# Where the rotated-partner copies of the first mixing linear stand in the request queue

## The reference, cut to what matters

```python
for l in range(DEPTH_2):                       # 2 layers
    h = rmsnorm(x, attn_norm[l])
    z = h @ w_in[l]                            # (512 x 1024) @ (1024 x 9420)
    (qA, kA, vA, fA, qB, kB, vB, qI, kI, wI,
     qC, kC, vC, gC, qD, kD, vD, gates) = jnp.split(z, split_at, axis=-1)
    yA = forgetting_attention(heads(qA, FOX_HEADS), ..., fA, forget_bias[l])
    yB = dsa_attention(rope(heads(qB, DSA_HEADS), pos), rope(kB[:, :, None], pos)[:, :, 0], vB,
                       rope(heads(qI, IDX_HEADS), pos), rope(kI[:, :, None], pos)[:, :, 0], wI)
    ...
    yD = sliding_window_gqa(rope(heads(qD, ...), pos), rope(heads(kD, ...), pos), heads(vD, ...), ...)
```

## Time and profile before

| | |
|---|---|
| median of three runs | 2974.98 us |
| the profiled execution, whole | 2973.03 us |
| its span, first to last instruction | 2971.2 us |
| mean granted TensorE clock | 0.998 |
| TensorE matmul busy | 2934.1 us (99% of the span) |
| VectorE busy | 1715.4 us (58%) |
| ScalarE busy | 1394.3 us (47%) |
| GpSimd busy | 1241.8 us (42%) |
| chain that ended last, by engine | TensorE 89%, VectorE 8%, ScalarE 2% |

### The profile page before, as it was taken

The page is one execution under the profiler, slowest core; times in us unless marked ns, Lnnn a source line. Parts: engine busy times, 40 slices in busy tenths (PEclk is TensorE's granted clock), DMA queues, the critical chain, the costliest instruction groups (busy, mean ns, idle before and its releaser), DMA issues.

```text
span 2971.2 us, 42626 instructions
## 1 busy us (share of the span) xinstructions
PE 2934.1 (99%) x16366; PEld 2454.2 (83%) x16366; DVE 1715.4 (58%) x2539; ACT 1394.3 (47%) x2318; POOL 1241.8 (42%) x870
## 2 busy tenths in 40 slices
PE   8999999999999999999999999999999999999998
PEld 7778888799988877788888888878787888878987
DVE  7974333497814978772117865178777511297732
ACT  6443344455533446663235545244566532354542
POOL 5336574410254533234555324454332354562243
PEclk9999999999999999999999999999999999999999
DMA  5334232233223422123323233244231233333322
GB/s 162 87 112 142 94 131 96 72 114 114 84 98 89 145 73 86 52 75 95 97 96 106 82 103 110 86 114 138 67 95 47 75 98 97 96 90 106 96 96 71
DMA packets 215047, 288.96 MB, mean 97 GB/s; under 512 B 42698, under 2 KB 122626, under 8 KB 213058
## 3 DMA queue, kind: packets, MB, share of 16 engines
q1 hardware_dynamic: 212354, 281.06, 31.2%
q0 software_dynamic: 880, 2.99, 0.3%
q10 hardware_dynamic: 1616, 2.23, 0.2%
HBM read 270.98 MB, written 4.72 MB: 93 GB/s over the span
## 4 chain that ended last, share of the span: by engine, by line
PE 89%; DVE 8%; ACT 2%; issue 1%; DMA 0%; POOL 0%; SPq 0%; ACTq 0%; DVEq 0%
PE half L914 69%; PE half L1243 3%; PE half L1246 3%; PE half L1245 3%; PE half L1402 2%; PE half L1416 2%; PE half L1380 1%; PE half L1385 1%; DVE arena L2546 1%; DVE arena L3523 1%; DVE qz L3523 1%; DVE arena L3037 1%; DVE wL L2569 1%; PE half L1478 0%; PE half L1169 0%
## 5 line engine op out<-in xcount | busy, mean ns | idle before, releaser
L3639 POOL TENSOR_TENSOR wL<-slot,wH 128x512 fp32r<-128x512 f32 (+1 forms) x840 | 1191.5, 1427 | 1700.2 <-ACT wH L1602 1665.5
L1602 ACT ACTIVATE wH<-slot 128x512 fp32r<-128x512 f32 (+1 forms) x840 | 515.9, 623 | 958.4 <-PE half L914 942.6
L914 PE MATMUL half<-arena_split,wH 128*128 128x512 f32 (+1 forms) x2432 | 736.0, 385 | 1.0 <-POOL wL L3639 0.6
L914 PE MATMUL half<-nH,wH 128*128 128x512 f32 x1792 | 709.5, 396 | 3.7 <-ACT arena L1615 2.3
L914 PE MATMUL half<-nH,wL 128*128 128x512 f32 x1792 | 698.6, 390 | 0.0
L914 PE MATMUL half<-nL,wH 128*128 128x512 f32 x1792 | 698.1, 390 | 0.0
L914 PEld LDWEIGHTS half<-arena_split,wH 128*128 128x128 f32 x2432 | 451.1, 188 | 93.8 <-POOL wL L3639 2.8
L914 PE MATMUL half<-arena_split,wL 128*128 128x512 f32 (+1 forms) x1216 | 466.4, 384 | 0.0
L914 PEld LDWEIGHTS half<-nH,wH 128*128 128x128 f32 x1792 | 336.4, 188 | 88.7 <-issue 18.2
L914 PEld LDWEIGHTS half<-nH,wL 128*128 128x128 f32 x1792 | 336.4, 188 | 71.6
L914 PEld LDWEIGHTS half<-nL,wH 128*128 128x128 f32 x1792 | 336.7, 188 | 67.9 <-issue 1.4
(11 more groups left out here) (424 smaller groups left out, 4542.4 us busy)
## 6 DMA issues: line engine op xcount, KB each, us to landing
slot<-in_w_in SPq DMA_DIRECT2D x344, 256.0 KB, 2.7
slot<-in_w_up SPq DMA_DIRECT2D x272, 128.0 KB, 2.2
slot<-in_w_down SPq DMA_DIRECT2D x132, 256.0 KB, 2.6
arena<-in_w_up SPq DMA_DIRECT2D x168, 128.0 KB, 2.4
slot<-in_w_branch SPq DMA_DIRECT2D x64, 256.0 KB, 2.7
slot<-in_w_out SPq DMA_DIRECT2D x48, 256.0 KB, 2.7
arena<-arena SPq DMA_DIRECT2D x40, 256.0 KB, 4.4
slot<-in_w_gate SPq DMA_DIRECT2D x48, 128.0 KB, 2.3
```

What stands on the lines that cost most here:

```text
L914: mm = pe.matmul(dst, lhsT, rhs, start=(k == 0 and m == 0), stop=(k == last and m == 2))
L1602: act.activation(wH[:, p, 0:cols], slot[:, s, 0:cols], ACT.Copy).then_inc(weights_high, 1)
L3639: pool.tensor_tensor(wL[:, p, 0:cols], slot[:, s, 0:cols], plainly(wH[:, p, 0:cols]), ALU.subtract)\
```

## The change

In each layer the four partner copies of `mix1` are asked for behind the first four units of `mix2` in place of behind all eight. Units 4 to 7 of `mix2` (sixteen requests) come behind the copies, ahead of qB units 4-7. The programs of the other four engines are the same.

```diff
                     load("b" + name, lin(w, r, c0), l, units=range(4))
+                    mix2 = cols((FOX_F, 8), (IDX_W, 4), (DSA_V, 64), (SWA_V, 128))
                     if name == "qB":
-                        load("bmix2", cols((FOX_F, 8), (IDX_W, 4), (DSA_V, 64), (SWA_V, 128)), l)
+                        load("bmix2", mix2, l, units=range(4))
                     if name in roped:
                         partners(*roped[name])
+                    if name == "qB":
+                        load("bmix2", mix2, l, units=range(4, KD))
                     load("b" + name, lin(w, r, c0), l, units=range(4, KD))
```

## The result

The changed kernel takes 2977.74 us (median of 21 runs, 2976.39 to 2980.14), the kernel before, in runs beside it, 2973.29 us (21 runs, 2972.28 to 2975.03). The ratio is 1.0014, 95% interval 1.0008 to 1.0021: slower, by 4.45 us between the medians. The forecast was +1.9 us and "no change". The time lies in the range, the sign and the place are as forecast, and the size is more than twice what was worked out; it is also just outside the "0.5 to 4" us that had most of the chance.

The account below looks back on a forecast made before the run. TensorE, busy for 99% of the span, was taken to bound the kernel. Losses of 1.7 us in layer 0 and 0.2 in layer 1, sum 1.9, on the median 2974.98 gave 2976.9 us; range 2974.0 to 2980.5.

Parts of the forecast that it names:

- 0.5 to 4: Whole kernel: the main forecast, slower by about 2 us within these limits in us; chance 0.72.
- The copies do not start earlier: SP, both layers: copy requests still begin when VectorE has emptied mix1, at 956.22 and 1970.34 us; gain 0.
- possible accident: Layer 1: VectorE's extra lag of 1.64 us behind the copy requests might come from traffic behind them; gain at most 1.50 us.
- What mix2 units 4-7 pay: Layer 0, behind the copies: sixteen requests at 0.475 us each make TensorE late at units 6, 7 and qB 4; 1.7 us.
- The bound of 2.4 for layer 0: Layer 0: upper bound of the loss in us, with GpSimd at 1.30 and 2.1 us for each subtraction.
- Layer 1 loses 0.2: Layer 1: the same 1.7 us late at qB unit 4, 1.5 covered; net 0.2 us, between -1.5 and 0.9.
- the 1.5 us of cover: Layer 1: TensorE already stood 1.50 us before index_dots, waiting for VectorE's rotation, so 1.5 us of lateness costs nothing.
- GpSimd blocked: Rival, units 6, 7 and qB 4: subtractions wait for whole VectorE operations of 2.2 us; 8.5 us in all, 2983.5; chance 0.05.
- The clock: Rival: new TensorE waits lower its granted clock in both layers, 1.7 us each; 2980.3 us; chance 0.03.
- SP held at every request: Rival: all sixteen requests take 1.20 us in place of 0.475; layer 0 11.7 late, layer 1 10.2; 2997 us; chance 0.02.
- Everything hidden: Rival: layer 0 loses 0.1, layer 1 nothing or gains up to 1.5; 2973.6 to 2975.1 us; chance 0.15.

Follow-up runs that it names:

- the two medians: The changed kernel timed twice against the kernel before, with no edit between: 2977.74 us beside 2973.29, then 2976.92 us beside 2973.52.

## Why the prediction was right in kind and short in size

**The copies do not start earlier: right.** They wait for VectorE's emptying of mix1 in both kernels. Their end does move, which the forecast took only for a possible accident. In layer 1 VectorE starts on them 8.55, 8.76 and 8.74 us after the first request in the three profiles in which that layer has the old order and undivided copies. It is 8.03, 8.22, 7.93 and 7.98 us in the four in which small pieces of mix2 stand right behind them. The most that index_dots had of this was 0.2 us, with the copies behind six units; with the copies behind four qB unit 4 came too late for it. Nor does what stands behind the copies land behind them: the first piece of mix2 in layer 1 is asked for at 1977.48 and lands 3.9 us later, at 1981.4, while VectorE waits for the copies until 1982.45.

**What mix2 units 4-7 pay: the mechanism was right, the size of layer 0 was not.** The worked sum said 1.7 us, and 2.8 was measured, in three profiles within 0.14 us. Unit by unit, units 5, 6 and 7 of mix2 and unit 4 of qB were to be 0, 0.6, 1.2 and 1.7 late, and were 1.4, 1.6, 1.8 and 2.8. The term that was too small is the request queue. I let SP be held twice just behind the copies and then go at 0.475 a piece. The request for the last piece of unit 5 was held a further 1.05 us. That made unit 5 late, which the prediction had as "just hidden", and all units behind it. GpSimd's 1.59 and 1.35 for units 4 and 5 against an assumed 0.63 and 0.85 did not matter but for 0.5 us at unit 5, since SP set the pace behind it. The bound of 2.4 for layer 0 was exceeded too: it had taken GpSimd at its slowest, but SP without another hold.

**Layer 1 loses 0.2: too small, by another term.** There the last piece of unit 7 is asked for 1986.09 - 1974.42 = 11.67 us after the first copy request, and the prediction had 967.9 - 956.22 = 11.7. What was off is GpSimd: 3.81 us for unit 7 and qB unit 4 where I took 1.1 + 1.5 = 2.6, with a pause of 0.3 between them. The narrow one waits for VectorE's operation that ends at 1989.63 and is over at 1990.10; the wide one waits for the next, which ends at 1991.18, and is over at 1992.32. So qB unit 4 is 2.7 late, not 1.7, and behind the 1.5 us of cover 1.2 is left, not 0.2. The cover itself was right. With these two terms put right the sum is 2.8 + 1.2 = 4.0, and the two medians are 4.45 and 3.40.

**The rivals.** GpSimd blocked (0.05): the mechanism was true and only its size was not. The prediction read the rows as "between no lock and a full one", and that reading was wrong. A subtraction waits for what is left of the operation under way, not for a whole one of 2.2 us: about 1.1 us each for the two in layer 1, which makes it 1.2 us late there in place of 5.0. In all twelve profiles the narrow subtractions that meet the rotation end 0.47 to 0.49 us after an operation of it (a few late ones, nearly past it, up to 0.60), and the wide ones 1.12 to 1.16 after. The Trainium skill, "SBUF — State Buffer", section "SBUF: two separate sides", says that whichever of the two starts first has the shared pair for the whole instruction and that the other fully blocks. The trace agrees. The clock (0.03): it did fall in layer 1, in one of two profiles of the changed kernel, at 1.6 us where the rows said 1.7. I had argued that the new waits were too small and too scattered; TensorE was busy for only 1.59 of 3.00 us, but so it was in the profile without the fall. SP held at every request (0.02): no, but one request in sixteen was held more than foreseen. Everything hidden (0.15): no; it is what happens with eight requests behind the copies.

## What to carry to other kernels

A request in a row of requests costs its issuing engine the same however few bytes it has, here 0.475 us from start to start for 2 to 256 KB. What matters when requests are moved is how many stand ahead of the first block that an engine wants, against how fast that engine uses blocks up. Before a wait is moved ahead of others, look at what ends it: this one ended at the same time wherever it stood, and only what was put behind it moved. Two engines that take turns must be counted as a pair: a subtraction of 0.63 us and a VectorE operation of 1.2 come every 1.56 us together, and that is slower than the 1.34 that TensorE needs. Where several small slacks follow each other (0.7 us at one unit, 0.2 at the next), put the bounds of all of their terms in the same direction for the upper end of the range.

## What the runs showed of the hardware that I had not expected

A request of 128 x 204 numbers takes SP as long as each of its four pieces does: three of them behind the copies in 2.84 us, two of which were held, and 0.90 for the pair of unit 7 and qB unit 4.

Some time after the copies, one more request of SP is held, by about 1 us: 1.96 and 1.85 us for a pair in place of 0.90 in the two profiles of the changed kernel in layer 0, both times at the end of mix2 unit 5; the pair begins 7.4 us after the first copy request. The place isn't fixed: with the copies ahead of all units it comes 15.5 us after the first copy request in layer 0 (1.32 us) and 10.2 after in layer 1 (1.84), and layer 1 of the changed kernel has none. It isn't the copies, the last of which has landed by then (VectorE starts on them at 6.93), nor a full DMA: the 16 engines are busy for 0.22 of the time from 965.40 to 966.60 us. The piece ahead of the held one lands after 3.0 us in place of 1.9. What SP waits for isn't shown in the profile and was not settled.

A fall of the granted clock costs nothing in the end if a later wait for weights is longer than what it cost: with the copies ahead of all units the clock was at 0.50 for six microseconds in layer 0 and at 0.51 for ten in layer 1, and qB unit 4 was as late as its requests made it.

GpSimd's subtractions and the rotation's operations on VectorE take turns, an instruction at a time, and both pay: VectorE's operation of line 3238 takes 1.22 us at 965.64, when it comes first, and 1.52 at 969.60, when a subtraction is under way until 970.03.
